# Two steps of the attention heads moved from VectorE to GpSimd: the running sum of softplus and the scaling of the forgetting heads' probabilities

## The reference, cut to what matters

```python
z = einsum('bhqd,bhkd->bhqk', qa, ka) * scale          # stick-breaking heads
log_not = where(strict, log_sigmoid(-z), 0.0)          # = -softplus(z)
rest = cumsum(log_not, reverse=True) - log_not         # over the keys behind this one
a_w = where(strict, exp(log_sigmoid(z) + rest), 0.0)
out_sb = a_w @ va

s = einsum('bhqd,bhkd->bhqk', qb, kb) * scale          # forgetting heads
s = s + c[..., q, None] - c[..., None, k]              # c: running sum of log forget gates
out_fox = softmax(where(causal, s, -inf)) @ vb
```

## Time and profile before

| what | before |
|---|---|
| time, median of 3 runs | 1788.49 us (1787.17 to 1789.54) |
| span of the profiled execution, first to last instruction | 1780.9 us |
| time of that execution outside its span | not listed; the median stands 7.6 us above the span |
| granted TensorE clock | 0.999 of full |
| TensorE busy over the span | 99% |
| VectorE / ScalarE / GpSimd busy over the span | 79% / 53% / 4% |

### The profile page before, as it was taken

How to read it: one execution, slowest core, us unless ns; L and a number is a source line. 1 busy time by engine, 2 the same in 40 slices (tenths; PEclk the granted TensorE clock), 3 DMA queues, 4 the chain that set the end, 5 groups by cost and what they waited for, 6 DMA issues and landing times.

```text
span 1780.9 us, 34402 instructions
## 1 busy us (share of the span) xinstructions
PE 1758.2 (99%) x13692; PEld 1702.0 (96%) x13692; DVE 1411.1 (79%) x2020; ACT 942.1 (53%) x1554; POOL 64.1 (4%) x168
## 2 busy tenths in 40 slices
PE   8999999999999999999999999999999999999998
PEld 8999999999987799999999999999999988899997
DVE  7857998779978857946998789469987688499975
ACT  5534655565567744533655545336555445266555
POOL 0000000002122201000000000000000000000000
PEclk9999999999999999999999999999999999999999
DMA  5242333326564422333343333333433323244332
GB/s 163 77 130 84 110 105 96 101 85 197 171 177 129 119 60 83 96 99 92 99 116 95 96 95 96 104 87 103 112 96 84 95 70 107 73 119 119 96 93 74
DMA packets 335157, 187.07 MB, mean 105 GB/s; under 512 B 18976, under 2 KB 325728, under 8 KB 335008
## 3 DMA queue, kind: packets, MB, share of 16 engines
q1 hardware_dynamic: 331568, 175.63, 35.6%
q0 software_dynamic: 2608, 8.72, 1.3%
q10 hardware_dynamic: 832, 0.62, 0.1%
HBM read 171.51 MB, written 10.82 MB: 102 GB/s over the span
## 4 chain that ended last, share of the span: by engine, by line
PE 84%; DVE 10%; issue 2%; ACT 2%; DMA 1%; POOL 0%; DVEq 0%; ACTq 0%; POOLq 0%; SPq 0%
PE pair L2570 47%; PE pair L2542 17%; PE pair L2511 8%; PE pair L2904 4%; PE pair L2557 1%; PE pair L840 1%; PE pair L2746 1%; DVE w_lo L2004 1%; DVE w_lo L1988 1%; PE pair L2833 1%; PE pair L2779 1%; DVE w_lo L1999 1%; PE pair L824 1%; PE pair L766 0%; DVE sums_w L1972 0%
## 5 line engine op out<-in xcount | busy, mean ns | idle before, releaser
L2570 PE MATMUL pair<-b_hi,w_hi 128*128 128x264 f32 (+1 forms) x1464 | 416.6, 285 | 2.2 <-DVE b_lo L2139 1.6
L2570 PE MATMUL pair<-b_hi,w_lo 128*128 128x264 f32 (+1 forms) x1464 | 414.6, 283 | 0.0
L2570 PE MATMUL pair<-b_lo,w_hi 128*128 128x264 f32 (+1 forms) x1464 | 414.6, 283 | 0.0
L2570 PEld LDWEIGHTS pair<-b_hi,w_hi 128*128 128x128 f32 x1464 | 275.8, 188 | 4.4 <-issue 2.9
L2570 PEld LDWEIGHTS pair<-b_lo,w_hi 128*128 128x128 f32 x1464 | 275.9, 188 | 0.0
L2570 PEld LDWEIGHTS pair<-b_hi,w_lo 128*128 128x128 f32 x1464 | 275.5, 188 | 0.0
L1506 ACT ACTIVATE w_hi<-sums_w 128x1024 fp32r<-128x1024 f32 x188 | 198.6, 1056 | 104.1 <-PE pair L2570 61.0
L1506 ACT ACTIVATE w_hi<-raw_all 128x1024 fp32r<-128x1024 f32 (+1 forms) x188 | 158.9, 845 | 141.4 <-PE pair L2570 100.0
L2570 PE MATMUL pair<-blocks_hi,w_hi 128*128 128x264 f32 (+1 forms) x816 | 231.7, 284 | 0.8 <-ACT parts L1689 0.8
L2570 PE MATMUL pair<-blocks_hi,w_lo 128*128 128x264 f32 (+1 forms) x816 | 231.2, 283 | 0.0
L2570 PE MATMUL pair<-blocks_lo,w_hi 128*128 128x264 f32 (+1 forms) x816 | 231.2, 283 | 0.0
(11 more groups left out here) (342 smaller groups left out, 3813.0 us busy)
## 6 DMA issues: line engine op xcount, KB each, us to landing
raw_all<-in_w_ffn_in SPq DMA_DIRECT2D x173, 512.0 KB, 4.0
raw_all<-in_w_ffn_out SPq DMA_DIRECT2D x64, 512.0 KB, 4.3
raw_all<-in_w_ffn_out SPq DMA_DIRECT2D x32, 384.0 KB, 3.6
raw_all<-in_w_attn_in SPq DMA_DIRECT2D x24, 512.0 KB, 4.4
qk_dram<-qk_hi POOLq DMA_DIRECT2D x16, 264.0 KB, 4.2
qk_dram<-qk_lo POOLq DMA_DIRECT2D x16, 264.0 KB, 2.9
raw_all<-in_w_attn_out SPq DMA_DIRECT2D x8, 512.0 KB, 4.9
head_v<-v_tok SPq DMA_DIRECT2D x16, 160.0 KB, 2.6
```

Of the source, the lines that this page charges most:

```text
L2570: mm = nc.tensor.matmul(dst, w[slot][:, c0 + kk * P:c0 + (kk + 1) * P], rhs(v, kk), start=(fresh and kk == 0 and w is w_hi and v == 0), st ...
```

## The change

The running sum and the scaling by the inverse sums leave VectorE's program and enter GpSimd's. GpSimd's step then is: mask softplus of this step, mask the weights of the step before, add softplus of the step before to `stick` (or the memset at s=0), scale this step's probabilities. VectorE waits before L1256 until `stick_ready` tells that the sum of the step before has been made, since L1256 overwrites the softplus that it read. In the first step the scaling stands directly behind the first softplus mask.

```diff
@@ VectorE: dve_scores @@
                 dve.wait_ge(ln_done, c + 1)
+                count_ge(dve, stick_ready, c)
                 nc.vector.scalar_tensor_tensor(softplus[g % 2][:, 0:w], ...)
@@ VectorE: dve_step @@
-                if s > 0:
-                    _, q1, nq = stick_tile(g - 1)
-                    count_ge(dve, sticks_done, c)
-                    dve.wait_ge(sp_masked, c)
-                    dve.wait_ge(stick_ready, c)
-                    if s == 1:
-                        nc.vector.tensor_tensor(stick[:, SEQ:T], stick[:, SEQ:T], softplus[(g - 1) % 2][:, nq:nq + META],
-                                                ALU.add).then_inc(stick_tail, 1)
-                        dve.wait_ge(stick_tail, 2 * hp + e + 1)
-                    nc.vector.tensor_tensor(stick[:, q1:T], stick[:, q1:T], softplus[(g - 1) % 2][:, 0:nq],
-                                            ALU.add).then_inc(stick_ready, 1)
@@ VectorE: dve_probs @@
                 nc.vector.reciprocal(stats[:, g % 2, 2:3], stats[:, g % 2, 1:2]).then_inc(p_inv, 1)
-                dve.wait_ge(p_inv, c + 1)
-                p = probs[s][:, 0:nk]
-                nc.vector.tensor_scalar(p, p, stats[:, g % 2, 2:3], None, ALU.mult).then_inc(p_done, 1)
@@ GpSimd @@
+                def stick_add(hp, g):
+                    e, s, c = g // 4, g % 4, STEPS * hp + g
+                    _, q1, nq = stick_tile(g - 1)
+                    before_ = softplus[(g - 1) % 2]
+                    wait_apart(pool, sticks_done, c)
+                    wait_apart(pool, sp_masked, c)
+                    wait_apart(pool, stick_ready, c)
+                    if s == 1:
+                        nc.gpsimd.tensor_tensor(stick[:, SEQ:T], stick[:, SEQ:T], before_[:, nq:nq + META],
+                                                ALU.add).then_inc(stick_tail, 1)
+                        wait_apart(pool, stick_tail, 2 * hp + e + 1)
+                    nc.gpsimd.tensor_tensor(stick[:, q1:T], stick[:, q1:T], before_[:, 0:nq],
+                                            ALU.add).then_inc(stick_ready, 1)
+
+                def probs_scaled(hp, g):
+                    wait_apart(pool, p_inv, STEPS * hp + g + 1)
+                    p = probs[g % 4][:, 0:fox_tile(g)[1]]
+                    nc.gpsimd.tensor_scalar(p, p, stats[:, g % 2, 2:3], None, ALU.mult).then_inc(p_done, 1)
+
                 softplus_mask(0, 0)
+                probs_scaled(0, 0)
                 pool.wait_ge(p5_done, ph.pairs[-1].s + 1)
                 nc.gpsimd.memset(v_tok[:, 1, QT - 1, :], 0.0).then_inc(v_pad, 1)
...
                         nc.gpsimd.memset(stick, 0.0).then_inc(stick_ready, 1)
+                    else:
+                        stick_add(hp, g)
+                    if not (first and g == 0):
+                        probs_scaled(hp, g)
```

## The result

The changed kernel takes 1790.13 us (median of 14 runs, 1788.80 to 1792.26), the kernel before in the same comparison 1786.55 us (14 runs, 1782.59 to 1789.54). The ratio is 1.0023 with a 95% interval of 1.0015 to 1.0031: a little slower, by 2.7 to 5.5 us. The prediction named 1790.8 us. It came that near by luck, with errors that cancel: the change cost more than the forecast 2.3 us, and it was added to a median that was too high.

What follows compares the result with a forecast made beforehand. TensorE, busy for 99% of the span, was taken as the bound. Step s=3 +1.2 and late first loads +1.1 made +2.3 us on the span of 1780.9, 1783.2; with 7.6 carried along 1790.8 us, 8-in-10 range 1785.5 to 1796.5.

Steps and rivals of the forecast that it cites:

- What bounds the kernel: TensorE, busy for 99% of the span; its idle 7.6 us in the heads are all that relieving VectorE can win.
- The rival in which VectorE's queue is the bound: In couples where VectorE has hardly a gap, both of TensorE's waits go: -4.6 us, 1783.9 us; chance 0.14.
- the one in which the low part gets in first: L1291 starts ahead of the addition: mask's 0.2 us won, -1.4 us, 1787.1 us if value loads are early; chance 0.14.
- The step s=3: Widest step of the heads: GpSimd's addition shuts out L1291, which ends 0.17 us later; seven couples make +1.2 us.
- The scalings: In the heads, GpSimd's scaling of 528 columns takes 0.64 us, is covered before TensorE's transposes and costs 0.
- the prediction's own list: Wrong if L1313 or L1291 start right behind VectorE, transposes L803 wait for GpSimd's scaling, or an addition exceeds 1.2 us.
- The staging of the first loads: First step: scaling ahead of four memsets starts them 1.62 us later; TensorE waits 1.1 us for values, +1.1 us once.
- The base of the sum: The span of 1780.9 us, plus the 7.6 us by which the median of the runs lies above it, carried along.

Runs made afterwards that it cites:

- the changed kernel without the staging delay: The changed kernel with the first scaling behind the memsets whose end SyncE waits for, not ahead of them: 1786.91 us, 1.0002 against the kernel before.
- the delay alone: The kernel before with nothing moved to GpSimd; only the memsets wait until VectorE has made the first scaling: 1789.59 us, 1.0020.

## Why the prediction was right and where it was wrong

**What bounds the kernel** was right. VectorE was relieved of 18 us and nothing came of it; before L1281 and L1300 it idles more than before, for ScalarE and TensorE. The rival in which VectorE's queue is the bound falls with that, and so does the one in which the low part gets in first: the addition is at work when L1281 begins.

**The step s=3** was right in mechanism and nearly in size. The low part ends 0.54 us behind the addition (forecast 0.53), by the exclusive lock that the Trainium skill, "SBUF — State Buffer", section "Who interferes with whom", has; with the addition moved away L1281 fell back to 0.69. Forecast +0.17 a couple, measured +0.22 in couples 4 to 7 and 0.9 us in couples 2 to 7. Only the profiles resolve this: the timing of the changed kernel without the staging delay, 1.0002, can't tell 1.2 us from nothing.

**The scalings** were mis-sized, 1.60 us for 0.64, because masks were taken for their neighbours, and their term was put at 0. By the prediction's own list (transposes that wait for them) that would make it wrong: the waits came, 2.8 us at L803 and 0.43 more before the last transposes. They cost nothing in couples 4 to 7, as the scaling alone shows. Part of them is taken off the later wait before L781, 0.4 us there; where the rest is made up the waits don't say. At the two ends of the heads they do cost: 0.7 us in the eighth couple, where nothing covers the last scaling, and 0.5 in the first.

**The staging of the first loads** is the largest step that was short. The forecast had +1.1 us. Alone it takes 1.0020 times the time before, 3.6 us (2.0 to 5.2; 3.0 between the medians), where the whole change takes 1.0023 times (4.1; 3.6). At the same mean clock it is 2.1 to 2.9 us. Three sizes were short: the memsets came 2.0 us later, not 1.62; the values 2.5, not 1.3; TensorE waited 1.6 and 2.1 us, not 1.1. And the prediction left the clock out: behind the wait TensorE ran partly at the lower level, which put 1.7 us on top in the profile here and 2.8 us in that of the delay alone. The Trainium skill, "TensorE: Matmul & The Clock Gate", section "HAM oscillation — how this bites in real kernels", tells of waits for DMA behind which the clock falls; the rows agree in kind, though the waits here are shorter than those it tells of. The prediction counted each wait of TensorE at its own length. What that misses is less in the medians than in the profiles, since the kernel before loses its clock as well: the mean clock is 0.9970 before (88 executions), 0.9964 with the delay alone and 0.9974 in the changed kernel.

**The base of the sum** was wrong as well. It carried 7.6 us from the span to the median, as if they lay outside the span. Over all executions here 1.7 to 2.5 us lie outside it (2.1 in the changed kernel). The rest was the clock: the trace read was of an execution with a mean clock of 0.999, and 1788.49 was a median of three others that were slower; over 14 runs it is 1786.55. (The forecast also puts VectorE's fixed part at 0.16 us, where its own rows give 0.18; nothing rests on it.) Of the 3.6 us between the medians the forecast had 2.3, and the base, 1.9 us too high, hid the rest. Executions of one clock differ more: at 0.997 it is 1791.5 us after (7 executions) against 1786.7 before (34), at 0.998 1790.0 (6) against 1784.7 (22), so some 5 us. Of these about 2 go when the first scaling stands behind the memsets; the other 3 are the sum and the scalings themselves, where the forecast had 1.2. The medians show less because the changed kernel's clock is a little higher. That its wait for the copy is 0.66 us in place of 1.06 would explain it, but isn't shown for this kernel.

**Open.** Why the same program keeps its clock in one execution and loses it in the next. The scaling alone behind the memsets costs 1.0014, and with the running sum moved as well 1.0002. That is the clock: at the same mean clock the first is some 2 us above before and the second 3, but their mean clocks are 0.9972 and 0.9985. Why these differ is open; the wait for the copy, 1.06 us against 0.66, would explain it, but was not varied by itself in that kernel. Some 1 us of the scaling's 2 lies in the first and the eighth couple; the rest wasn't located. And whether the copy ahead of the sum gains its 0.1%.

## What to carry to other kernels

When an instruction moves to another engine's queue, look first at what stands behind it there and what that releases: here four memsets, and behind them all the loads of the stage. A wait of one or two microseconds on a TensorE that is otherwise dense can cost about double in one execution, since the clock may fall behind it. Price an operation by the same operation on the same engine or treat it as unknown, look at the first and the last pass of a loop by themselves, and compare traces and medians only with their mean granted clocks beside them: two kernels can have level medians and differ by 3 us at the same clock.

## What the runs showed of the hardware

- GpSimd's multiplication by a scalar is slower than its addition of two tiles: 2.5 against 2.1 ns a column, float32. Its selection and memset take 0.8 to 0.9.
- A VectorE subtraction of 512 columns with both inputs in SBUF that started during a GpSimd addition ended 0.54 us behind the addition's end, 1.10 us after its own start; alone it took 0.69.
- GpSimd was lengthened in its turn: its addition of 400 columns took 1.32 us in place of 1.03 beside VectorE's scaling of 528 columns (0.50 us).
- TensorE fell to 0.50 of its clock for 3 us and more behind waits of 1 to 2 us between busy stretches, in some executions and not in others; in single profiles also behind one of 0.65 us and behind three of 0.3 to 0.5 us close together. The time of the kernel before goes with it: some 1.6 us for each thousandth of the mean clock.
